# Modulation products of the first feed-forward moved from TensorE to VectorE

## What is computed

```python
cond = jax.nn.silu(c)
for i in range(DEPTH):
    mod = cond @ mod_w[i] + mod_b[i]          # 1024 -> 6 * 1024
    sh1, sc1, g1, sh2, sc2, g2 = jnp.split(mod, 6, axis=-1)
    h = modulate(rms_norm(x, norm_mix_g[i]), sh1, sc1)
    x = x + g1[:, None, :] * mixer(h)
    h = modulate(rms_norm(x, norm_ffn_g[i]), sh2, sc2)
    x = x + g2[:, None, :] * conv_ffn(h, ...)

def conv_ffn(h, w_up, conv_w, conv_b, w_down):
    z = causal_depthwise_conv(h @ w_up) + conv_b      # 3 taps, 2 * 2816 channels
    val, gate = jnp.split(z, 2, axis=-1)
    return (jax.nn.silu(gate) * val) @ w_down
```

## Time and profile before

| what | value |
|---|---|
| median of 3 runs | 767.09 us (766.11 to 768.42) |
| profiled execution, own time | 767.76 us |
| its span, first to last instruction | 765.8 us |
| mean granted TensorE clock | 0.984 |
| PE busy | 727.7 us, 95% |
| DVE busy | 530.4 us, 69% |
| ACT busy | 411.9 us, 54% |
| POOL busy | 127.7 us, 17% |

### The profile page before, as it was taken

How to read it: one execution, slowest core, us unless ns; L and a number is a source line. 1 busy time by engine, 2 the same in 40 slices (tenths; PEclk the granted TensorE clock), 3 DMA queues, 4 the chain that set the end, 5 groups by cost and what they waited for, 6 DMA issues and landing times.

```text
span 765.8 us, 17216 instructions
## 1 busy us (share of the span) xinstructions
PE 727.7 (95%) x6636; PEld 660.5 (86%) x6636; DVE 530.4 (69%) x897; ACT 411.9 (54%) x682; POOL 127.7 (17%) x120
## 2 busy tenths in 40 slices
PE   4789999999999999999999999989999999999996
PEld 1478999457888999999999799979969999999995
DVE  4756665995488788777867686556567767676665
ACT  4244644565465556675567653325556555555554
POOL 1000000211015343434303254430000000000000
PEclk9799999999999999999999999989999999999998
DMA  8979755696755767667676041008725555555521
GB/s 315 378 272 383 255 190 165 255 406 246 283 215 182 280 187 257 209 238 238 221 260 204 3 138 58 29 29 342 263 73 192 177 183 174 192 191 165 192 83 56
DMA packets 46068, 156.61 MB, mean 205 GB/s; under 512 B 6016, under 2 KB 7312, under 8 KB 46016
## 3 DMA queue, kind: packets, MB, share of 16 engines
q1 hardware_dynamic: 43344, 148.26, 55.2%
q10 hardware_dynamic: 2160, 6.38, 2.2%
q0 software_dynamic: 512, 1.25, 0.4%
HBM read 154.82 MB, written 1.05 MB: 204 GB/s over the span
## 4 chain that ended last, share of the span: by engine, by line
PE 85%; DVE 7%; issue 3%; ACT 3%; POOL 1%; DMA 1%; DVEq 0%; POOLq 0%; ACTq 0%
PE up L368 13%; PE up L370 13%; PE up L369 13%; PE acc L368 9%; PE acc L369 9%; PE acc L370 9%; PE gv L410 5%; DVE wlo L1165 2%; PE misc L469 1%; PE up L752 1%; DVE tmp L1193 1%; PE up L765 1%; PE acc L740 1%; DMA ident<-in_ident 1%; PE acc L498 1%
## 5 line engine op out<-in xcount | busy, mean ns | idle before, releaser
L1165 DVE TENSOR_TENSOR wlo<-raw,whi 128x1024 fp32r<-128x1024 f32 x188 | 252.7, 1358 | 77.2 <-ACT whi L820 70.8
L368 PE MATMUL up<-hh,whi 128*128 128x256 f32 x896 | 255.7, 285 | 1.9 <-DVE hl L1198 1.9
L370 PE MATMUL up<-hh,wlo 128*128 128x256 f32 x896 | 253.5, 283 | 0.0
L369 PE MATMUL up<-hl,whi 128*128 128x256 f32 x896 | 253.5, 283 | 0.0
L820 ACT ACTIVATE whi<-raw 128x1024 fp32r<-128x1024 f32 x185 | 192.5, 1051 | 41.0 <-PE acc L370 26.3
L368 PEld LDWEIGHTS up<-hh,whi 128*128 128x128 f32 x896 | 171.7, 192 | 9.8 <-issue 3.8
L369 PEld LDWEIGHTS up<-hl,whi 128*128 128x128 f32 x896 | 171.8, 192 | 0.0
L370 PEld LDWEIGHTS up<-hh,wlo 128*128 128x128 f32 x896 | 171.8, 192 | 0.0
L1496 DVE SCALAR_TENSOR_TENSOR ffn<-up,conv,ffn 128x254 f32<-128x254 f32 (+1 forms) x176 | 72.7, 475 | 45.6 <-ACT ffn L1015 45.3
L368 PE MATMUL acc<-ah,whi 128*128 128x256 f32 x352 | 99.8, 284 | 0.6 <-DVE wlo L1165 0.6
L369 PE MATMUL acc<-al,whi 128*128 128x256 f32 x352 | 99.6, 283 | 0.0
(11 more groups left out here) (240 smaller groups left out, 920.6 us busy)
## 6 DMA issues: line engine op xcount, KB each, us to landing
raw<-in_w SPq DMA_DIRECT2D x188, 512.0 KB, 3.4
mraw<-in_mw SPq DMA_DIRECT2D x48, 512.0 KB, 6.1
arena<-in_mw SPq DMA_DIRECT2D x24, 512.0 KB, 9.7
raw<-in_w SPq DMA_DIRECT2D x12, 256.0 KB, 13.0
tmp<-in_mw SPq DMA_DIRECT2D x6, 512.0 KB, 7.7
ffn<-in_mw SPq DMA_DIRECT2D x6, 512.0 KB, 8.5
tmp<-in_mw ACTq DMA_DIRECT2D x4, 512.0 KB, 6.0
ffn<-in_mw ACTq DMA_DIRECT2D x4, 512.0 KB, 8.6
```

Of the source, the lines that this page charges most:

```text
L368: pe.matmul(out, w_h, xh, start=first, stop=False, skip_group_check=skip)
L369: pe.matmul(out, w_h, xl, start=False, stop=False, skip_group_check=skip)
L370: return pe.matmul(out, w_l, xh, start=False, stop=last, skip_group_check=skip)
L1165: dve.tensor_tensor(wlo[:, n % SPL, :], raw[:, n % RAW, :], whi[:, n % SPL, :].bitcast(F32), ALU.subtract).then_inc(lo_ready, 1)
```

## The change

Chunks 16 to 19 are no longer made by PE. Their weights are laid out transposed on the host, so that a block of 128 x 1024 holds 128 outputs on the partitions and the 1024 inputs along the row. A row of `c`, repeated on all partitions (`condrow`, 512 KB), is loaded into the free tile `tmp` and put through Silu by ACT (`crow`). DVE multiplies a block with it and sums along the row in one instruction (`dot`), one block in each of the steps 4 to 19, between the split of c+2 and the gate; after eight blocks it adds the bias. Chunk 20 stays with PE and is made ahead of the first double step, and the `row_out` that it waits for moves ahead of ACT's feed-forward. Two `row_out`, `columns` and `col_out` go. SP waits for the end of the norm before it loads `crow`, and for each dot before it loads the next block. `made` and `rows` correct the counts.

```diff
+DOTS = 4
+def made(c):
+    return c - DOTS if isinstance(c, int) and c >= C_FFN + DOTS else c
+def rows(pair):
+    return pair - DOTS // 2 if isinstance(pair, int) and 2 * pair >= C_FFN + DOTS else pair
...
+        crow = tmp8[:, 0:1024]
...
-            load_m(C_FFN, own=C_OUT)
-            with sp_.Fori(0, 4) as i:
-                for n in range(W_FFN0 + RAW, W_FFN0 + 3 * RAW):
-                    load_w(n, 2 * i)
-                load_m(C_FFN + 1, i)
-            for n in range(W_FFN0 + 9 * RAW, W_FFN0 + 11 * RAW):
+            load_m(C_SIN - 1, own=C_OUT)
+            sp_.wait_ge(act_lo, 3 * KT)
+            sp_.dma_start(crow, t["condrow"]).then_inc(crow_in, 16)
+            for n in range(W_FFN0 + RAW, W_FFN0 + 2 * RAW):
                 load_w(n)
-            load_m(C_SIN)
+            load_m(C_FFN, own=C_SIN - 1)
+            for n in range(W_FFN0 + 2 * RAW, W_FFN0 + 3 * RAW + 3):
+                load_w(n)
+            with sp_.Fori(0, DOTS - 1) as i:
+                for s in range(MS):
+                    sp_.wait_ge(dot_done, MS * i + s + 1)
+                    sp_.dma_start(mraw[:, s, :], t["mw"][(C_FFN + 1 + i) * MS + s, :, :]).then_inc(m_loaded[s], 16)
+                    for n in range(3 * s, 3 * s + 3):
+                        load_w(W_FFN0 + 3 * RAW + 3 + n, 2 * i)
...
                 if layer == 0:
+                    gemv(C_SIN - 1)
                     two_steps(0, (C_OUT // 2, 0))
-                    with pe.Fori(0, 2) as i:
-                        gemv(C_FFN, i)
-                        two_steps(4 * i + 1)
-                        two_steps(4 * i + 2)
-                        gemv(C_FFN + 1, i)
-                        two_steps(4 * i + 3, (C_FFN // 2, i))
-                        two_steps(4 * i + 4)
-                    gemv(C_SIN - 1)
-                    two_steps(9)
+                    with pe.Fori(1, 10) as i:
+                        two_steps(i)
...
-                    two_steps(0, (C_OUT // 2, 0))
-                    for i in range(2):
...
+                    two_steps(0)
+                    act.wait_ge(crow_in, 16)
+                    act.activation(crow, crow, ACT.Silu).then_inc(crow_ready, 1)
+                    for i in range(1, 9):
+                        two_steps(i)
...
             act.wait_ge(small_in, 16 * N_SMALL)
+            row_out(C_OUT // 2)
             ffn_phase(0, W_FFN0)
...
+                def dot(n, i):
+
+                    dve.wait_ge(m_loaded[n % MS], 16 * (C_FFN // 2 + 1 + n // MS + 2 * i))
+                    dve.wait_ge(crow_ready, 1)
+                    src = mraw[:, n % MS, :]
+                    dve.scalar_tensor_tensor(src, src, 1.0, crow, ALU.mult, ALU.mult,
+                                             accum_out=modc[:, ds(4 * C_FFN + n + 8 * i, 1)]).then_inc(dot_done, 1)
+                    if n == 7:
+                        dve.wait_ge(dot_done, 8 * (i + 1))
+                        pair = modc[:, ds(4 * C_FFN + 8 * i, 8)]
+                        dve.tensor_tensor(pair, pair, modb[:, ds(4 * C_FFN + 8 * i, 8)], ALU.add).then_inc(mod_col, 1)
...
                     conv_rest(h, s, off + s)
                     if c + 2 < N_SLOTS:
                         split_lo(c + 2, i)
+                    if product is not None:
+                        dot(*product)
                     gate(h, off + s)
                     low(h, off + s)
```

More of the change, by code:

```diff
@@ L283, in load_m @@
                     if own is not None:
-                        sp_.wait_ge(mod_used, own * MS + s + 1)
+                        sp_.wait_ge(mod_used, made(own) * MS + s + 1)
                     elif not (isinstance(c, int) and isinstance(i, int) and c + i == 0):
@@ L334, in _ @@
                 load_w(n)
-            load_m(C_FFN, own=C_OUT)
-            with sp_.Fori(0, 4) as i:
-                for n in range(W_FFN0 + RAW, W_FFN0 + 3 * RAW):
-                    load_w(n, 2 * i)
-                load_m(C_FFN + 1, i)
-            for n in range(W_FFN0 + 9 * RAW, W_FFN0 + 11 * RAW):
-                load_w(n)
-            load_m(C_SIN)
+            load_m(C_SIN - 1, own=C_OUT)
+            sp_.wait_ge(act_lo, 3 * KT)
+            sp_.dma_start(crow, t["condrow"]).then_inc(crow_in, 16)
+            for n in range(W_FFN0 + RAW, W_FFN0 + 2 * RAW):
+                load_w(n)
+            load_m(C_FFN, own=C_SIN - 1)
[7 more added lines that the diff above has]
+                        load_w(W_FFN0 + 3 * RAW + 3 + n, 2 * i)
+            for s in range(MS):
+                if s < 3:
+                    for n in range(3 * s, 3 * s + 3):
+                        load_w(W_FFN0 + 9 * RAW + 3 + n)
+                sp_.wait_ge(dot_done, MS * (DOTS - 1) + s + 1)
+                sp_.dma_start(mraw[:, s, :], t["mw"][C_SIN * MS + s, :, :]).then_inc(m_loaded[s], 16)
             for n in range(W_SIN, W_GLU + RAW + 3):
@@ L385, in gemv @@
                 if c >= 2 and not odd and slots[0] == 0:
-                    pe.wait_ge(gm_ready, c // 2 + i)
+                    pe.wait_ge(gm_ready, rows(c // 2) + i)
                 for s in slots:
@@ L395, in gemv @@
                     elif c >= C_FFN:
-                        pe.wait_ge(m_loaded[s], 16 * (c - C_FFN // 2 + 2 * i))
+                        pe.wait_ge(m_loaded[s], 16 * (C_FFN // 2 if c < C_SIN else C_FFN // 2 + 1 + DOTS))
                     elif c == 0:
@@ L415, in columns @@
             def columns(pair, i=0):
-                pe.wait_ge(gm_ready, pair + i + 1)
+                pe.wait_ge(gm_ready, rows(pair) + i + 1)
                 if pair:
@@ L462, in norm @@
                 if pairs:
-                    pe.wait_ge(gm_ready, pairs)
+                    pe.wait_ge(gm_ready, rows(pairs))
                     pe.wait_ge(mod_col, pairs)
@@ L710, in transpose_b @@
                 if mt == 0:
-                    pe.wait_ge(gm_ready, C_GLU // 2)
+                    pe.wait_ge(gm_ready, rows(C_GLU // 2))
                 if mt:
@@ L822, in row_out @@
             def row_out(pair, i=0):
-                act.wait_ge(mod_used, 2 * MS * (pair + i + 1))
+                act.wait_ge(mod_used, 2 * MS * (rows(pair) + i + 1))
                 if pair:
-                    act.wait_ge(cols_done, pair + i)
+                    act.wait_ge(cols_done, rows(pair) + i)
                 act.activation(gm[:], gv[:], ACT.Copy).then_inc(gm_ready, 1)
@@ L1168, in col_out @@
             def col_out(pair, i=0):
-                dve.wait_ge(cols_done, pair + i + 1)
+                dve.wait_ge(cols_done, rows(pair) + i + 1)
                 if pair >= 2:
@@ L1172, in col_out @@
                     dve.tensor_reduce(gsum[:].rearrange("p (e q) -> p e q", e=2), parts, AX.X, ALU.add).then_inc(part_sum, 1)
-                    dve.wait_ge(part_sum, pair + i - 1)
+                    dve.wait_ge(part_sum, rows(pair) + i - 1)
                     dve.tensor_tensor(modc[:, ds(8 * (pair + i), 8)], gsum[:], modb[:, ds(8 * (pair + i), 8)],
@@ L1508, in ffn_phase, with step @@
                 off = FT * layer
-                def step(h, s, c, i=0, extra=None):
+                def dot(n, i):
[8 more added lines that the diff above has]
+                        dve.tensor_tensor(pair, pair, modb[:, ds(4 * C_FFN + 8 * i, 8)], ALU.add).then_inc(mod_col, 1)
+                def step(h, s, c, i=0, extra=None, product=None):
                     conv_rest(h, s, off + s)
@@ L1532, in ffn_phase, with two_steps @@
                 split_lo(base + 7)
-                def two_steps(i, extra=None):
+                def two_steps(i, extra=None, product=None):
                     for h in range(2):
-                        step(h, 2 * i + 2 + h, base + 6 + 3 * h, i, extra if h else None)
+                        step(h, 2 * i + 2 + h, base + 6 + 3 * h, i, extra if h else None,
+                             product and (product[0] + h, product[1]))
                 if layer == 0:
@@ L1539, in ffn_phase @@
                     with dve.Fori(0, 2) as i:
[L1540 to L1543, removed]
+                        for j in range(4):
+                            two_steps(4 * i + 1 + j, None, (2 * j, i))
                 else:
@@ L1852, in layout @@
     mw = mod_w.reshape(2, MS, 2, P, CH, 512).transpose(0, 4, 1, 3, 2, 5).reshape(2 * CH * MS, P, 1024)
+    for c in range(C_FFN, C_FFN + DOTS):
+        part = mod_w[c // CH][:, 512 * (c % CH):512 * (c % CH) + 512]
+        mw[c * MS:(c + 1) * MS] = part.T.reshape(MS, P, D)
     q = np.arange(P)[:, None]
@@ L1861, in layout @@
         "cond": _columns(i["c"][0]),
+        "condrow": np.repeat(i["c"][0][None], P, axis=0),
         "modb": _columns(mod_b).reshape(P, 96),
```

9 lines of the change are left out of this document (3 added, 6 removed).

## The result

The changed kernel takes 771.14 us (median of 12 runs, 768.52 to 771.87) where the kernel before, run beside it, took 766.49 us (765.29 to 768.42): 4.65 us more by the medians; the ratio is 1.0052, 1.0041 to 1.0064, which is 3.1 to 4.9 us. The forecast was +5.4 us and 772.5 us. The profiled execution took 769.64 us, with a span of 767.7 us; before it was 767.76 with 765.8.

The account below looks back on a forecast made before the run. PE bounds the kernel, busy 95%; with dots DVE sets the pace of steps with POOL. 15.4 us lost less 9.6 gained is +5.8, less about 0.4 slack: +5.4, 772.5 us; own range 769.5 to 779, wider range 764 to 781.

Parts of the forecast that it names:

- Gain on PE: Four products (7.3 us) and two `columns` (0.9) leave PE, 1.4 of chunk 20's product is hidden: 9.6 us gained.
- Chunk 20's product: Moved ahead of the first pair of steps, where PE waits for `wlo`: 1.4 of its 1.83 us hidden.
- The dot: Sixteen on DVE, steps 4 to 19, between split and gate: 1.28 us each, bounds 1.13 and 1.5.
- Rival A: Dot on DVE runs at half rate, 1.07 us more in all sixteen steps: +22.5, 789.5 us; chance 0.12.
- The step: DVE's step with POOL: 8.46 + 1.28 = 9.74 us, 1.10 above PE; 15.4 us lost over steps 4 to 17.
- POOL's share: What POOL's operations add to a DVE step, mostly at the two last splits: 1.56 us in seven steps.
- The pads: ACT's 2.18 us operations after seven steps, ahead of the next `chain_a`: some 2 us more, in the upper bound only.
- Rival B: Dot hidden, DVE's step stays under 8.64 us, the whole 9.6 us come out: 757.5 us; chance 0.08.
- Rival C: POOL costs DVE only 1.04 us a step, step 9.22 us: -1.5, 765.6 us; chance 0.14.
- The sign that was named for both: DVE still waiting for ACT's `tap` by a microsecond in mid-phase would make the prediction wrong, pointing to B or C.
- a clean step: DVE's step without POOL's work: 6.9 + 1.28 = 8.2 us, under PE's 8.64, so the dot is hidden.
- Parts 3 and 4: The 512 KB row's load and Silu, and SP's new load order: nothing; late block at most 6.1 us, once.

Follow-up runs that it names:

- e1: Changed kernel with each dot over 16 of its 1024 columns, loads, waits and order kept: 755.3 us, 0.9853 of the kernel before.
- e6: Changed kernel with both POOL's multiplications (16 of 512 columns) and ACT's pads (1 of 32 groups) cut short: 756.04 us, 0.9857 of the kernel before.
- e5: Changed kernel with ACT's pads copying 1 of 32 groups, dots and POOL's work whole: 767.01 us, 1.001 of the kernel before.
- e2: Changed kernel with POOL's multiplications over 16 of 512 columns, dots whole, pads kept: 761.75 us, 0.9927 of the kernel before.
- e7: Changed kernel, complete, with POOL's operations released by the last split of a step instead of by `low`: 767.08 us, 1.0005 of the kernel before.
- e11: Changed kernel, complete, with POOL released by the last split and the dot moved behind that split: 759.75 us, 0.9917 of the kernel before.
- e4: Changed kernel, complete, with the dot moved from ahead of the gate to between the last two splits: 771.04 us, 1.0053 of the kernel before.

## Why the prediction was right

**Gain on PE, forecast 9.6 us.** L433 has 16 matmul records in the whole phase, at 223.1, as foretold. With the dots' cost out of the way the kernel is 11.3 us (e1) and 11.0 us (e6) faster than before; the interval of e1 begins at 9.7 us. The profiled executions give 10.3, inside that interval: from the last `hl` to the end of the phase it is 188.3 us in e1 and 198.6 before. PE's timelines tell where the 0.7 us over the forecast come from. Beside its own 1.83 us a product costs some 0.2 more, as PE loses a little at both of its edges: the group of `acc` matmuls ahead takes 2.97 us in place of 2.88, the group of `up` matmuls behind 5.86 in place of 5.76. The forecast had the 1.83 alone. Chunk 20's product was rightly taken as hidden by 1.4 of its 1.83 us: with it, PE reaches the place of chunk 16's product 26.9 us behind the last `hl`, for 26.4 before, 0.5 later.

**The dot, forecast 1.28 us.** It is 1.14 from start to start. The form and the sum cost nothing over the split (1217 ns against 1.21 us), and the read of the accumulator, priced at 0.09, lies beside the start of the gate. With 1.14 the forecast's own sum would have been 14 x 0.96 = 13.4, less 9.6 and 0.4: +3.4. *Rival A* (half rate, 2.2 us) is refuted by the same rows. (The Trainium skill, Vector Engine (DVE) Microarchitecture Reference, section 7, gives this form half its throughput with two SBUF sources that are not bf16; these runs show 1217 ns for 1024 elements, no loss, and so the measurement decides against it. That the read of the accumulator is an instruction of its own is in the Trainium skill, VectorE: DVE Perf Modes, section on two Vector instructions with no wait between them; the trace agrees, with 16 records of 81 ns.)

**The step, forecast 9.74 us.** It is 9.67, both over the fourteen steps counted and over fifteen, 9.39 to 9.91. But the forecast's own terms come to less. The dot is 1.14 and not 1.28. POOL's share is 1.47 and not 1.56: the two last splits take 3.82 us in the mean of the fourteen steps, and 8.46 was the mean of the seven steps with most of POOL. So 6.9 + 1.14 + 1.47 = 9.51, and e5, in which the pads are short, has 9.53 over these steps. With that the forecast would have been 14 x 0.89 = 12.5, less 9.6 and 0.4: +2.5. The pads, put at nothing, bring the 3.2 us of e5. The loss of 15.3 us by e1, forecast 15.0, is thus in part luck: two terms too large and one left out cancel. *Rival B* is refuted: the step is a microsecond above PE's. *Rival C* is refuted in its step (9.22) and its time (765.6), and right in that POOL's share is not whole in every step; a split's mean is 1687 ns from 245 to 395 us, against 1565. The sign that was named for both, a wait of DVE for the tap by a microsecond in the middle of the phase, did come, once; and it is neither's, for the wait stands behind a pad:
```profile
342.83 2.90 DVE L1182 TENSOR_TENSOR wlo<-raw,whi 128x1024 fp32r<-128x1024 f32 x2 [0.52 <-ACT whi L837]
346.87 1.65 DVE L1513 SCALAR_TENSOR_TENSOR ffn<-up,conv,ffn 128x255 f32<-128x255 f32 x4 [1.14 <-ACT ffn L1032]
```

**The step that was wrong inside the right sum.** The working said that a clean step, 6.9 + 1.28 = 8.2 us, hides the dot, and it priced ACT's pads as an upper bound only (2 us). e2 shows that without POOL each step after a pad still takes 9.73. In most steps POOL's ring alone is nearly as long (9.62), so it shows little in the total. It shows by itself in step 18, which POOL no longer disturbs and which the prediction called clean and hidden: the splits are at 2.36 us, and the step from 385.23 to 394.96 still takes 9.73.
```profile
390.91 2.36 DVE L1182 TENSOR_TENSOR wlo<-raw,whi 128x1024 fp32r<-128x1024 f32 x2 [0.52 <-ACT whi L837]
394.96 1.65 DVE L1513 SCALAR_TENSOR_TENSOR ffn<-up,conv,ffn 128x255 f32<-128x255 f32 x4 [1.68 <-ACT ffn L1032]
```
The pad stood in the earlier trace rows, but what ACT does ahead of and behind it was not added up: 8.59 us without the dot, so that all of the dot but 0.05 us makes such a step longer than PE's. Seven of the sixteen steps with a dot have a pad; with POOL's share gone a part of the loss would have stayed, 4.0 us of PE's waits in e2.

**Parts 3 and 4, forecast nothing.** No load comes late: e1 keeps them all and PE has no wait. The phase took 5.2 us more, forecast 5.4; PE's waits come 14 times and are 0.2 to 1.1 us in the timeline, forecast 0.5 to 1.3, but for one of 1.77.

## What to carry to other kernels

When work is moved to an engine with idle time, ask of each idle stretch what ends it. If the end is released, over another engine, by this engine's own earlier instruction, the stretch is a link of a ring, and only what is put behind the release and ahead of the wait fits into it: with POOL's later pace the same change took 1.0005 of the time before with the dot ahead of the gate (e7) and 0.9917 with it behind the last split (e11). When two rings are nearly equal, remove both in one experiment as well as each alone, with a control on the kernel before; otherwise each looks cheap. And look where the control's gain lies: here it was in another stretch than the one in question.

## What the runs showed of the hardware

**Of a dot and a POOL operation, the one that starts second waits for the end of the first.** Dot behind POOL: 2.08 us in the median in place of 1.22 (e4). POOL behind the dot: 1.91 in place of 1.06 (e11). Beside a DVE operation with one operand in PSUM neither is longer (e7: 1.65 for four, 1.06). (The Trainium skill, SBUF — State Buffer, "Who interferes with whom", says that a VectorE instruction with two SBUF inputs contends with a GpSimd instruction that reads SBUF, and that the order of issue decides which of them is blocked; the rows agree.)

**The granted clock fell in the changed kernel's phase, once.** Stretches of after (columns as in the earlier trace rows) and the PE timeline there:
```profile
322.00:326.00 4.00, 2.23 (x19) 2.03 (x18) 3.10 (x3) 4.00 (x6) 2.99 (x2) 1.00 0.69 222
326.00:330.00 4.00, 4.00 (x23) 4.00 (x22) 4.00 (x7) 0.51 (x2) 0.21 (x1) 0.57 0.71 249
330.00:334.00 4.00, 4.00 (x36) 4.00 (x36) 3.00 (x5) 2.43 (x4) 1.40 (x2) 1.00 0.69 232
```
```profile
325.35 0.39 PE L391 MATMUL acc<-ah,whi 128*128 128x256 f32 x1 [1.77 <-DVE wlo L1182]
...
326.62 0.42 PE L391 MATMUL acc<-ah,whi 128*128 128x256 f32 x1
326.83 0.42 PE L392 MATMUL acc<-al,whi 128*128 128x256 f32 x1
```
PE waited 1.77 us for `wlo`, the longest of the 14 waits, and about a microsecond later its matmuls follow each other at 0.21 us in place of 0.12: the lower of the clock's two levels, 1.2 GHz (granted clock 0.50 from 326.4 to 329.8 us), for some 3 us; the slice of 4 us shows 23 matmuls for 36. The longest wait stands in the step in which DVE also adds the bias to the first eight columns, 0.29 us between dot and gate. The next step on DVE, in which the clock was low, is 9.91 us, against 9.73 for the longest others without such an addition, so the low clock cost at most some 0.2 us here, where DVE sets the pace. Behind the other waits the clock stayed up (up to 1.14 us here, up to 1.30 in e7). That the long wait brought it down is likely by this order of time, and no run tried it.
